# A decoder step on one core: the projection's three groups run as one loop, an exponential is put ahead of weight loads, and a cache copy's 16 runs lie far apart

## The chip, the core and the metric

The kernel runs on one NeuronCore of a Trainium2 chip. TensorE (PE) multiplies into PSUM, VectorE (DVE) and ScalarE (ACT) work elementwise, GpSimd (POOL) copies and broadcasts. SyncE (SP), ACT and POOL issue DMAs, and all of them run on the core's 16 DMA engines. The engines run apart and meet at semaphores. The metric is the device time of one execution in microseconds (us); before the change the median of three runs is 1215.42 us (1214.69 to 1216.04).

## The reference, cut to what matters

One inference step of a two-layer decoder trunk over 256 prompt tokens and 8 sample tokens, width 1024, all in float32:

```
layer 0: u = rms_norm(h)
         z = u @ w_qkv            # 1024 -> 3 groups x (q, k, v) x 16 heads x 64
         q, k = rms_norm per head # v is left as it is
         prompt: banded dilated attention per group, merged over groups
         sample: per group, the new q against 128 cached keys (every 1st, 4th, 16th row
                 of a cache of 128, 512, 2048 rows) and its own k; softmax; times v
         h += merged @ w_o
         new caches = the old caches moved on by one row, the new k and v as last row
layer 1: h += pooling mixer(rms_norm(h))
each layer: route every token to 2 of 16 experts; h += sum of gate * expert(rms_norm(h))
```

The three sample caches are outputs too: 8 samples x (128, 512, 2048) rows x 2 x 1024 floats, each row but the last taken from the input cache one row further on. That is about 176 MB read and written by DMA, with no arithmetic in it.

## The kernel before, in words

**Stages.** In order of time: the norm of the input; the projection; the attention of the 8 samples; the attention of the prompt, one head after another; the product with `w_o`; router and experts of layer 0; the pooling mixer; router and experts of layer 1; the outputs. Each engine has its own program, written out by hand; Python loops are unrolled, `Fori` is a loop on the engine.

**Projection** (PE L1061, ACT L625, DVE L781, POOL L460). A group g has 24 tiles of 128 columns: 8 of q (n = 0 to 7), 8 of k, 8 of v. For a tile PE runs 8 matmuls over the width (L1074); for q and k ACT squares (L629), PE sums the squares per head (L1083), ACT takes the root (L635), DVE the reciprocal and the product (L791, L792); v tiles are only copied (L796). Three tiles behind, PE transposes the result (L1092, L1093) and ACT stores it (L647 to L651); POOL keeps q and k for the prompt's attention (L480). PE, ACT and DVE each run `Fori` over the groups, and a group's body ends when its own last tile is through: PE waits until ACT has stored tile 23 (L1094), DVE until PE has turned it (L805). The next group's tile 0 starts after that. The weights come in chunks of four tiles through three ring slots: SP loads chunk c when PE is done with chunk c - 3 (L372).

**Scores of the samples.** Beside tiles n = 14 to 21, DVE multiplies sample b = n - 14's cached keys with its query, spread over the partitions by POOL, and sums per head (L797 to L804). POOL loads sample b + 4's keys and spreads query b + 2 once sample b is scored (L491 to L496). After the last group, PE adds up the scores (L1103 to L1105) and DVE finds their maximum (L822 to L824).

**Softmax of the samples.** ACT loads the new v rows (L657) and the router's weights (L659, L660: four DMAs whose runs are 4 or 16 floats), and then takes the exponential (L662). DVE divides (L826 to L829), PE turns the result (L1109, L1110), DVE masks it (L832 to L835). PE then adds the new rows' part (`p_newT`, L1114) and the cached values' part in two halves of three loads each (L1123). SP issues half 1's loads into the slots of half 0 as PE frees them (L384).

**Cache copies.** 168 DMAs from the input caches to the output caches: 1, 4 or 16 pieces for each sample. A piece is `[16, y]`: 16 runs of y elements, one for each DMA engine: 65,024, 65,408 or 65,504 bytes by cache. SP puts them between its loads, and a table of counts says how many after which load: L268, here in the order of use:

```
5 and 7 after the first chunks, 3 after each chunk, 2 after each of two value loads of half 0 ("last_chunks"),
2 after half 0, 3, then 1 or 2 per head, 3, 4, 14 before the router, 1 or 2 per expert pair of layer 0,
28 in the pooling stage, 2 per pair of layer 1, the rest (9) after the last expert load
```

SP's queue keeps this order, so a load stands behind the copies issued before it. SP ends when the outputs and all copies have landed (L451, L452).

**Experts** (L1252). Eight pairs of experts per layer; a pair needs six loads of 2 MB (gate, up, down for two experts) in six slots, and a slot's next load is issued when PE has used the old one (L426 to L430).

Of the kernel before, what the change touches and what calls it, by code (L numbers as in the profile page):

```python
# [5 lines left out]
ALU = mybir.AluOpType  # L6
# [4 lines left out]
ds = bass.ds  # L11

P = 128
# [30 lines left out]
def build(nc, x_prompt, x_sample, cache_w128, cache_w512, cache_w2048, state_pool, w_qkv, q_norm,  # L44
# [40 lines left out]
    with ExitStack() as ctx:  # L85
# [251 lines left out]
        def _(sp):  # L337
# [118 lines left out]
        def _(pool):  # L456
# [3 lines left out]
            for g in range(G):  # L460
# [3 lines left out]
                def spread_q(b):  # L464
                    at = 32 * (b // 3 + 1)

                    if b % 2 == 0 and b <= 2:
                        pool.wait_ge(zn_kept, g * NQK + (NQK - 2 + b))
# [7 lines left out]
                for n in range(NQK):  # L476
                    pool.wait_ge(zn_ready, g * NZ + n + 1)
                    if n == KT + 6:
                        pool.wait_ge(q_spread, g * NS + 2)
# [7 lines left out]
                    if n == KT + 5:  # L487
# [20 lines left out]
                pool.wait_ge(rows_sent, g * 16 + 16)  # L508
# [88 lines left out]
        def _(ac):  # L597
# [27 lines left out]
            with ac.Fori(0, G) as g:  # L625
                for s in range(NZ + 4):
                    if s < NQK:
                        ac.wait_ge(z_ready, g * NZ + (s + 1))
                        nc.scalar.activation(zsq[:, s % 2, :], z_bank[s % 4][:, 0:T], ACT.Square).then_inc(zsq_ready, 1)  # L629
                    if 1 <= s <= NQK:  # L630
                        n = s - 1
                        ac.wait_ge(zsum_ready, g * NQK + (n + 1))
                        if n >= 2:
                            ac.wait_ge(zn_ready, g * NZ + (n - 1))
                        nc.scalar.activation(zr[:, n % 2, :], bank[2 + n % 2][:, 0:T], ACT.Sqrt, bias=epsc[:, 0:1],  # L635
                                             scale=1.0 / HD).then_inc(zroot_ready, 1)
                    if s >= 4:
                        n = s - 4
                        what, k = n // KT, n % KT
                        at = slice(k * P, (k + 1) * P)  # L640
                        src = bank[4 + n % 2]
                        if n == 0:
                            ac.wait_ge(tokens_sent, g * (16 * SENT_PER_G) + 16)
                        ac.wait_ge(z_turned, g * NZ + (n + 1))
                        if what == 1:
                            for b in range(2):
                                nc.scalar.activation(k_tok[b][:, at], src[:, b * P:(b + 1) * P], ACT.Copy)  # L647
                        if what == 2:
                            nc.scalar.activation(v_tok[:, :, ds(g, 1), at].rearrange("p b a c -> p (b a) c"),
                                                 src[:, 0:2 * P].rearrange("p (b c) -> p b c", b=2), ACT.Copy)  # L650
                        nc.scalar.activation(qkv_s[0:NS, what, at], src[0:NS, 2 * P:3 * P], ACT.Copy).then_inc(z_stored, 1)  # L651


# [98 lines left out]
        def _(dve):  # L752
# [28 lines left out]
            with dve.Fori(0, G) as g:  # L781
                chain.enter(g, NQK + 1 + NS)
                chain(vec.tensor_copy(gains[:], vecs[:, ds(g * 2 + QK_G, 2)]))
                for n in range(NZ):
                    if n >= 4:
                        dve.wait_ge(z_turned, g * NZ + (n - 3))
                        if n - 4 < NQK:
                            dve.wait_ge(zn_kept, g * NQK + (n - 3))
                    if n < NQK:
                        dve.wait_ge(zroot_ready, g * NQK + (n + 1))  # L790
                        chain(vec.reciprocal(zri[:, n % 2, :], zr[:, n % 2, :]))  # L791
                        vec.scalar_tensor_tensor(out=zn[:, n % 4, :], in0=z_bank[n % 4][:, 0:T], scalar=gains[:, n // KT:n // KT + 1],  # L792
                                                 in1=zri[:, n % 2, :], op0=ALU.mult, op1=ALU.mult).then_inc(zn_ready, 1)
                    else:
                        dve.wait_ge(z_ready, g * NZ + (n + 1))
                        vec.tensor_copy(zn[:, n % 4, :], z_bank[n % 4][:, 0:T]).then_inc(zn_ready, 1)  # L796
                    b = n - (NZ - 2 - NS)  # L797
                    if 0 <= b < NS:
# [612 lines left out]
```

## Time and profile before

| | |
|---|---|
| median of 3 runs | 1215.42 us |
| the profiled execution | 1215.45 us, of it 1213.7 us from the first to the last instruction |
| PE busy | 1090.1 us (90% of the span) |
| DVE, POOL, ACT busy | 434.7, 243.1, 217.1 us |
| DMA | 462.51 MB, mean 381 GB/s |
| the chain that ended last | PE 49%, DMA 14%, DVE 5% |
| 168 copies, issue to landing | medians of 18.4 to 22.1 us by cache |

"Busy" of PE is modelled: its matmuls overlap, and a PE that waits within a stage still shows up as idle only in the rows of that stage. The share of the DMA engines counts the time of their packets, so it may pass 1.00, and a packet that is slowed by others counts for longer. So for DMA the bytes per second of a stretch are read beside its share. Times of rows are us from the start of the span.

### The profile page before, as it was taken

To read this page: it belongs to the slowest core of one execution; us is meant where nothing else is said; L and a number is where in the kernel's file an instruction comes from. 1 tells how busy PE (TensorE), PEld (TensorE's weight loads), DVE (VectorE), ACT (ScalarE), POOL (GpSimd) and SP (SyncE) were. 2 spreads that over 40 slices of the span, in tenths; PEclk is the share of its full clock that TensorE was granted. 3 is DMA by queue.
4 is the path that set the end of the run, shared out by engine and by line. 5 is a ranking of instruction groups with operands and counts; after the bars stand their busy time and mean duration, and the time that the engine had idled before them with its cause. 6 is when DMAs were issued, how large, how long until landed. Compare 5 with 4: busy or idle time off the path is not lost.

```text
span 1213.7 us, 14577 instructions
## 1 busy us (share of the span) xinstructions
PE 1090.1 (90%) x4927; PEld 657.5 (54%) x4927; DVE 434.7 (36%) x843; ACT 217.1 (18%) x532; POOL 243.1 (20%) x504
## 2 busy tenths in 40 slices
PE   7998799999945899997999999998569799999995
PEld 4787588888831588763434444444433344443443
DVE  3455455835840367323112212113851122211212
ACT  2221122222200234212011111112111111111110
POOL 1014202421420122003122222220213221112220
PEclk9999899999976699996999999999678999999998
DMA  9999997999895999999999999999999999999998
GB/s 366 349 382 377 406 364 274 389 372 400 303 370 181 391 344 353 371 355 346 373 430 429 439 416 430 429 438 418 377 331 327 434 424 427 431 429 434 429 432 277
DMA packets 61888, 462.51 MB, mean 381 GB/s; under 512 B 11196, under 2 KB 19148, under 8 KB 46836
## 3 DMA queue, kind: packets, MB, share of 16 engines
q1 hardware_dynamic: 49136, 440.29, 92.4%
q0 software_dynamic: 5424, 18.75, 4.2%
q10 hardware_dynamic: 7284, 2.87, 1.0%
q8 instruction: 30, 0.49, 0.2%
q14 instruction: 14, 0.11, 0.0%
HBM read 454.99 MB, written 183.21 MB: 526 GB/s over the span
## 4 chain that ended last, share of the span: by engine, by line
PE 49%; DMA 14%; DVE 5%; issue 2%; ACTq 1%; ACT 1%; SPq 0%; DVEq 0%; POOLq 0%
PE bank L1262 22%; DMA ring_lo<-in_w_up_dram 12%; PE bank L1232 7%; PE bank L1286 3%; PE bank L1185 2%; DMA ring_lo<-in_cache_kv_w_dram 2%; PE bank L1144 1%; PE bank L1164 1%; PE bank L1241 1%; PE bank L1152 1%; PE bank L1141 1%; PE bank L1248 1%; PE bank L296 1%; PE bank L1192 1%; PE bank L1123 1%
## 5 line engine op out<-in xcount | busy, mean ns | idle before, releaser
L1262 PE MATMUL bank<-ring_lo,scratch 128*64 128x512 f32 x1024 | 340.6, 599 | 11.2 <-DMA ring_lo<-in_w_up_dram 9.3
L1074 PE MATMUL bank<-uT,ring_lo 128*128 128x264 f32 x1152 | 273.7, 392 | 3.2 <-ACT scratch L651 2.7
L1074 PEld LDWEIGHTS bank<-uT,ring_lo 128*128 128x128 f32 x1152 | 218.0, 194 | 43.9 <-issue 4.6
L1262 PE MATMUL bank<-region_a,scratch 128*64 128x512 f32 x512 | 227.8, 598 | 0.0
L1262 PEld LDWEIGHTS bank<-ring_lo,scratch 128*64 128x64 f32 x1024 | 107.0, 138 | 149.7 <-issue 149.3
L791 DVE RECIPROCAL scratch<-scratch 128x264 f32<-128x264 f32 x48 | 86.5, 1802 | 106.0 <-ACT scratch L635 106.0
L1232 PE MATMUL bank<-scratch 128*128 128x512 f32 (+1 forms) x216 | 119.0, 679 | 3.1 <-DVE scratch L947 3.1
L1262 PEld LDWEIGHTS bank<-region_a,scratch 128*64 128x64 f32 x512 | 67.8, 137 | 65.9 <-issue 64.0
L972 DVE TENSOR_TENSOR scratch<-bank,scratch 128x512 f32<-128x512 f32 x16 | 11.1, 692 | 246.8 <-PE bank L1262 246.8
L979 DVE TENSOR_TENSOR hT<-bank,hT 128x264 f32<-128x264 f32 x128 | 55.4, 432 | 120.0 <-PE bank L1286 118.6
L542 POOL TENSOR_TENSOR small<-epsc 128x1 f32<-128x1 f32 x71 | 13.8, 194 | 374.2 <-PE bank L1248 358.8
L1232 PEld LDWEIGHTS bank<-scratch 128*128 128x128 f32 (+1 forms) x216 | 37.7, 201 | 81.1 <-issue 79.5
L480 POOL COPY region_a<-scratch 128x264 f32<-128x264 f32 x48 | 24.6, 512 | 192.1 <-DVE scratch L792 191.8
L1286 PE MATMUL bank<-scratch 128*128 128x264 f32 x256 | 61.2, 392 | 0.0
L556 POOL TENSOR_SCALAR scratch<-slot_no,scratch 128x64 f32<-128x64 f32 (+1 forms) x108 | 60.5, 579 | 0.8 <-issue 0.3
L1286 PEld LDWEIGHTS bank<-scratch 128*128 128x128 f32 x256 | 47.3, 190 | 20.3 <-issue 13.0
L726 ACT ACTIVATE scratch<-bank 128x512 f32<-128x512 f32 x18 | 10.8, 597 | 242.8 <-PE bank L1232 242.8
L629 ACT ACTIVATE scratch<-bank 128x264 f32<-128x264 f32 x48 | 18.7, 391 | 158.5 <-PE bank L1074 145.8
L802 DVE TENSOR_TENSOR ring_lo<-ring_lo,scratch 128x1024 f32<-128x1024 f32 x24 | 40.9, 1706 | 14.9 <-POOL scratch L472 7.9
L562 POOL TENSOR_SCALAR scratch<-slot_no,scratch 128x64 f32<-128x64 f32 (+1 forms) x108 | 44.8, 430 | 0.0
L472 POOL PARTITION_BROADCAST scratch<-scratch x24 | 33.0, 1373 | 37.6 <-DVE scratch L803 23.7
L740 ACT ACTIVATE scratch<-bank 128x512 f32<-128x512 f32 x32 | 19.1, 597 | 93.3 <-PE bank L1262 93.3
(226 smaller groups left out, 1116.7 us busy)
## 6 DMA issues: line engine op xcount, KB each, us to landing
out_dram<-in_cache_kv_w_dram SPq DMA_DIRECT2D x128, 1023.5 KB, 22.1
ring_lo<-in_w_up_dram SPq DMA_DIRECT2D x32, 2048.0 KB, 22.4
ring_lo<-in_w_qkv_dram SPq DMA_DIRECT2D x18, 2048.0 KB, 17.1
ring_lo<-in_w_gate_dram SPq DMA_DIRECT2D x16, 2048.0 KB, 14.7
region_a<-in_w_down_dram SPq DMA_DIRECT2D x16, 2048.0 KB, 15.2
region_a<-in_w_gate_dram SPq DMA_DIRECT2D x16, 2048.0 KB, 19.9
ring_lo<-in_w_down_dram SPq DMA_DIRECT2D x16, 2048.0 KB, 19.4
out_dram<-in_cache_kv_w_dram SPq DMA_DIRECT2D x32, 1022.0 KB, 18.4
```

The costliest lines, as they stand in the source:

```text
L472: nc.gpsimd.partition_broadcast(q_rep[b % 2][:, :], q_row[at:at + 1, b % 3, :], channels=P).then_inc(q_spread, 1)
L480: nc.gpsimd.tensor_copy(qk[:, g, n // KT, n % KT, :], zn[:, n % 4, :]).then_inc(zn_kept, 1)
L556: last = nc.gpsimd.tensor_scalar(pick_gate[0:n, b, e * CAP:(e + 1) * CAP], slot_no[0:n, :], pair_at[0:n, 0, b, e:e + 1], pair_at[0:n, 1, b ...
L562: last = nc.gpsimd.tensor_scalar(pick[0:n, b, e * CAP:(e + 1) * CAP], slot_no[0:n, :], pair_at[0:n, 0, b, e:e + 1], None, ALU.is_equal)
L791: chain(vec.reciprocal(zri[:, n % 2, :], zr[:, n % 2, :]))
L802: chain(vec.tensor_tensor(k_tile, k_tile, q_rep[b % 2][:, :], ALU.mult))
L979: vec.tensor_tensor(hT[:, m, :], spread_bank[m % 4][:, 0:T], hT[:, m, :], ALU.add).then_inc(spread_added, 1)
L1074: last = mm(z_bank[s % 4][:, 0:T], w[:, k, at:at + P], uT[:, k, :], start=(k == 0), stop=(k == KT - 1))
L1185: last = mm(bank[m % 2][:, 0:T], w[:, f % 4, m * P:(m + 1) * P], oT[:, f, :], start=(f == 0), stop=(f == KT - 1))
L1232: last = mm(bank[a][:, :], made[0:sizes[b], b, :], u_tok[0:sizes[b], b, a * 512:(a + 1) * 512], start=(b == 0), stop=(b == 2))
L1262: last = mm(out[rows, :], lhs[:, k, rows], weights[e][w][:, k, columns], start=(k == 0), stop=(k == k_tiles - 1))
L1286: mm(spread_bank[m % 4][:, 0:T], y_pair[:, m * P:(m + 1) * P], place, start=True, stop=True).then_inc(spread, 1)
```

## The change

The projection's `Fori` loops become one unrolled loop over 72 tiles on PE, ACT and DVE. Tile i's buffers are chosen by i, so that tile 0 of the next group follows tile 23, and the transposes, roots and stores of a group's last tiles come after the first matmuls of the next. The waits at a group's end go; ACT waits for the transfers that read its token buffers only where it writes them again. The scores of sample b move from tile n = 14 + b to n = 16 + b, and POOL spreads the queries one tile later.

ACT takes the samples' exponential ahead of the loads of the new v rows and the router's weights. PE adds the new rows' part between the two halves, as eight matmuls of 32 columns in place of two of 128. POOL no longer waits for its own store of v before it stores the new cache row.

"last_chunks" goes from 2 to 3, so two more copies are issued at the end of the projection, and 7 in place of 9 are left for the end. A copy piece is cut differently: for the cache of 2048 rows, its 16 runs began 65,504 bytes apart, and now begin 16 x 65,504 = 1,048,064 bytes apart; for 512 rows 65,408 and now 261,632; for 128 rows there is one piece per sample and nothing changes. The bytes of a piece and its 16 runs stay as long as they were.

```diff
-        COPIES = {"first_chunks": 7, "chunk": (3, 3, 3), "last_chunks": 2, "sample_half": (2, 0), "head": (1, 2), "heads_end": 3,
+        COPIES = {"first_chunks": 7, "chunk": (3, 3, 3), "last_chunks": 3, "sample_half": (2, 0), "head": (1, 2), "heads_end": 3,
...
-                moved.append([v[0].rearrange("b l w h e -> b (l w h e)")[:, at:at + m].rearrange("b (n x y) -> b n x y", n=n, x=16)
+                moved.append([v[0].rearrange("b l w h e -> b (l w h e)")[:, at:at + m].rearrange("b (x n y) -> b n x y", n=n, x=16)
...
-                pool.wait_ge(rows_sent, g * 16 + 16)
...
-            with ac.Fori(0, G) as g:
-                for s in range(NZ + 4):
+            for i in range(TILES + 4):
...
+                    if n % NZ == KT:
+                        ac.wait_ge(tokens_sent, g * (16 * SENT_PER_G) + 16)
...
+            ac.wait_ge(s_rows_ready, 1)
+            nc.scalar.activation(s_rows[:, :, :], s_rows[:, :, :], ACT.Exp, bias=small[:, 36:37],
+                                 accum_out=small[:, 37:38]).then_inc(s_exp_ready, 1)
             ac.wait_ge(rows_sent, 16 * G)
...
-            ac.wait_ge(s_rows_ready, 1)
-            nc.scalar.activation(s_rows[:, :, :], s_rows[:, :, :], ACT.Exp, bias=small[:, 36:37],
-                                 accum_out=small[:, 37:38]).then_inc(s_exp_ready, 1)
...
-                    b = n - (NZ - 2 - NS)
-                    if 0 <= b < NS:
+                b = n - (NZ - NS)
+                if b >= 0:
...
-                dve.wait_ge(z_turned, g * NZ + NZ)
-                dve.wait_ge(zn_kept, g * NQK + NQK)
...
-            with pe.Fori(0, G) as g:
-                for s in range(NZ + 3):
+            for i in range(TILES + 3):
...
-                pe.wait_ge(z_stored, g * NZ + NZ)
...
-            pe.wait_ge(v_new_landed, 16)
-            for a in range(2):
-                mm(bank[3 + a][:, :], p_newT[0:G * NS, :], v_new[0:G * NS, a * 512:(a + 1) * 512], start=True, stop=False)
...
+                if half == 0:
+                    pe.wait_ge(v_new_landed, 16)
+                    for a in range(2):
+                        for b4 in range(HALF):
+                            rows = slice(b4 * 2 * H, (b4 + 1) * 2 * H)
+                            mm(bank[3 + a][rows, :], p_newT[0:G * NS, rows], v_new[0:G * NS, a * 512:(a + 1) * 512], start=False, stop=False)
```

PE at the end of a group, before: the last tile's matmuls (L1074), the transposes of the tiles still under way (L1092, L1093), and the branch back that waits for ACT's last store.

```order
L1074 MATMUL bank7<-uT,ring_lo 128x264 [waits zn_ready]
L1074 MATMUL bank7<-uT,ring_lo 128x264 x7
L1086 REGISTER_ALU
L1092 MATMUL bank4<-ident,scratch 128x128 [waits z_stored,zn_ready]
...
L1092 MATMUL bank5<-ident,scratch 128x128 [waits z_stored,zn_ready]
L1092 MATMUL bank5<-ident,scratch 128x128
L1093 MATMUL bank5<-ident,scratch 8x128
L1061 REGISTER_ALU [waits z_stored]
L1061 COMPARE_AND_BRANCH
```

The same place now (the matmuls are L1082, the transposes L1100 and L1101, the sum of squares L1091):

```order
L1082 MATMUL bank7<-uT,ring_lo 128x264 [waits zn_ready]
L1082 MATMUL bank7<-uT,ring_lo 128x264 x7
L1100 MATMUL bank4<-ident,scratch 128x128 [waits z_stored,zn_ready]
L1100 MATMUL bank4<-ident,scratch 128x128
L1101 MATMUL bank4<-ident,scratch 8x128
L1082 MATMUL bank0<-uT,ring_lo 128x264 [waits zn_ready,ring_full0]
L1082 MATMUL bank0<-uT,ring_lo 128x264 x7
L1100 MATMUL bank5<-ident,scratch 128x128 [waits z_stored,zn_ready]
L1100 MATMUL bank5<-ident,scratch 128x128
L1101 MATMUL bank5<-ident,scratch 8x128
```

Tile 0 of the next group (bank0) now stands between the transposes of the last tiles, and no branch or wait for the last store stands ahead of it.

ACT after the projection, before: the load of the new v rows (L657), four loads of router weights, then the table load and the exponential of the samples' scores (L662).

```order
L657 DMA scratch<-v_of_samples 24x1024 [waits z_turned,zn_kept,rows_sent]
L659 DMA wr<-in_router_group_w_dram 128x8x4
L660 DMA wr<-in_router_expert_w_dram 128x8x16
L659 DMA wr<-in_router_group_w_dram 128x8x4
L660 DMA wr<-in_router_expert_w_dram 128x8x16
L662 ACT_TABLE_LOAD
L662 ACTIVATE rstd,small<-rstd,small 128x387 [waits s_rows_ready]
```

And now:

```order
L664 ACT_TABLE_LOAD
L664 ACTIVATE rstd,small<-rstd,small 128x387 [waits s_rows_ready]
L669 DMA scratch<-v_of_samples 24x1024 [waits z_turned,zn_kept,rows_sent]
L671 DMA wr<-in_router_group_w_dram 128x8x4
L672 DMA wr<-in_router_expert_w_dram 128x8x16
L671 DMA wr<-in_router_group_w_dram 128x8x4
L672 DMA wr<-in_router_expert_w_dram 128x8x16
```

The table load and the exponential have moved past five DMAs; the table load itself waits for nothing.

PE in the samples' attention, before: the turned probabilities (L1109, L1110), the new rows' part (L1114), and the first matmuls of half 0 (L1123).

```order
L1109 MATMUL bank1<-ident,rstd 128x128 x2
L1110 MATMUL bank2<-ident,ring_lo 24x128
L1114 MATMUL bank3<-scratch,ring_lo 128x512 [waits v_new_landed,p_keys_ready]
L1114 MATMUL bank4<-scratch,ring_lo 128x512
L1123 MATMUL bank3<-ring_lo 32x512 [waits ring_full0]
```

And now, up to the first load of half 1 (L1128 is L1123 of before, L1136 the new rows' part):

```order
L1118 MATMUL bank2<-ident,ring_lo 24x128
L1128 MATMUL bank3<-ring_lo 32x512 [waits ring_full0,p_keys_ready]
...
L1128 MATMUL bank4<-ring_lo 32x512 x4
L1136 MATMUL bank3<-scratch,ring_lo 32x512 [waits v_new_landed]
L1136 MATMUL bank3<-scratch,ring_lo 32x512 x3
L1136 MATMUL bank4<-scratch,ring_lo 32x512 x4
L1128 MATMUL bank3<-ring_lo 32x512 [waits ring_full0]
```

The new rows' part has moved behind all of half 0, and with it the wait for the new v rows.

## Rows read from the trace of the kernel before

**Rows 1.** The page: busy tenths of PE and DMA, and GB/s, in 40 slices.

```profile
PE   7998799999945899997999999998569799999995
...
DMA  9999997999895999999999999999999999999998
GB/s 366 349 382 377 406 364 274 389 372 400 303 370 181 391 344 353 371 355 346 373 430 429 439 416 430 429 438 418 377 331 327 434 424 427 431 429 434 429 432 277
```

**Rows 2.** Five stretches: length, busy of PE, PEld, DVE, ACT, POOL; PE clock, DMA share, GB/s.

```profile
150.00:240.00 90.00, 90.00 (x429) 75.88 (x428) 61.33 (x55) 20.83 (x71) 22.50 (x31) 1.00 0.92 349
325.00:404.00 79.00, 47.32 (x232) 26.90 (x230) 24.91 (x39) 6.03 (x19) 12.24 (x18) 0.73 0.82 295
425.00:500.00 75.00, 73.38 (x530) 62.66 (x529) 49.37 (x171) 32.35 (x93) 15.79 (x22) 0.99 1.01 342
860.00:920.00 60.00, 40.77 (x139) 23.35 (x141) 31.47 (x106) 11.00 (x22) 10.53 (x28) 0.72 1.00 335
965.00:1171.00 206.00, 201.60 (x852) 86.41 (x852) 37.36 (x72) 27.51 (x42) 41.89 (x108) 0.99 1.01 429
```

**Rows 3.** PE's order of time in the projection: start, length, line; idle before, its releaser.

```profile
92.99 3.73 PE L1074 MATMUL bank<-uT,ring_lo 128*128 128x264 f32 x16
...
97.32 3.73 PE L1074 MATMUL bank<-uT,ring_lo 128*128 128x264 f32 x16
...
101.21 3.73 PE L1074 MATMUL bank<-uT,ring_lo 128*128 128x264 f32 x16
...
109.62 4.81 PE L1074 MATMUL bank<-uT,ring_lo 128*128 128x264 f32 x16
...
114.60 3.73 PE L1074 MATMUL bank<-uT,ring_lo 128*128 128x264 f32 x16
...
122.38 3.73 PE L1074 MATMUL bank<-uT,ring_lo 128*128 128x264 f32 x16
...
127.19 3.73 PE L1074 MATMUL bank<-uT,ring_lo 128*128 128x264 f32 x16
...
139.92 10.33 PE L1074 MATMUL bank<-uT,ring_lo 128*128 128x264 f32 x32 [1.35 <-ACT scratch L651]
...
150.54 3.72 PE L1074 MATMUL bank<-uT,ring_lo 128*128 128x264 f32 x16
...
236.82 3.73 PE L1074 MATMUL bank<-uT,ring_lo 128*128 128x264 f32 x16
...
251.59 3.72 PE L1074 MATMUL bank<-uT,ring_lo 128*128 128x264 f32 x16
```

**Rows 4.** DVE's order of time: the first score of group 0.

```profile
103.06 2.20 DVE L802 TENSOR_TENSOR ring_lo<-ring_lo,scratch 128x1024 f32<-128x1024 f32 x1 [7.35 <-POOL scratch L472]
```

**Rows 5.** DVE's order of time: either side of the samples' exponential.

```profile
354.93 0.15 DVE L824 TENSOR_SCALAR small<-small 128x1 f32<-128x1 f32 x1
369.04 0.16 DVE L826 RECIPROCAL small<-small 128x1 f32<-128x1 f32 x1 [13.95 <-ACT rstd L662]
```

**Rows 6.** ACT's order of time there (ACTq: its queue issues a DMA).

```profile
354.14 9.30 ACTq L659 DMA_DIRECT2D wr<-in_router_group_w_dram  x1
...
367.00 1.28 ACT L662 ACT_TABLE_LOAD   x1 [20.83 <-issue]
```

**Rows 7.** PE's order of time in the samples' attention.

```profile
372.26 3.77 PE L1114 MATMUL bank<-scratch,ring_lo 24*128 24x512 f32 x4 [0.90 <-DVE ring_lo L835]
375.96 8.06 PE L1123 MATMUL bank<-ring_lo 128*32 128x512 f32 x48
...
392.42 3.23 PE L1123 MATMUL bank<-ring_lo 128*32 128x512 f32 x16 [2.38 <-DMA ring_lo<-in_cache_kv_w_dram]
397.54 1.92 PE L1123 MATMUL bank<-ring_lo 128*32 128x512 f32 x16 [1.88 <-DMA ring_lo<-in_cache_kv_w_dram]
```

**Rows 8.** Waits of the whole run: us in total, times, longest.

```profile
PE bank L1262 <- DMA ring_lo<-in_w_up_dram: 9.3, 5, 5.1
```

**Rows 9.** Waits of SP's queue, in the same form.

```profile
SPq L452 <- DMA out_dram<-in_cache_kv_w_dram: 7.7, 1, 7.7
```

More of the change, by code:

```diff
@@ L465, in spread_q @@
                     at = 32 * (b // 3 + 1)
[L467 to L468 removed]
+                    if b in (0, 2):
+                        pool.wait_ge(zn_kept, g * NQK + (NQK if b else NQK - 1))
                     if b >= 1:
@@ L622, in _ @@
             ac.wait_ge(bias_stored, 16)
-            with ac.Fori(0, G) as g:
-                for s in range(NZ + 4):
[L627 to L651, printed above, removed]
@@ new lines, in _ @@
+            for i in range(TILES + 4):
+                if i < TILES and i % NZ < NQK:
+                    ac.wait_ge(z_ready, i + 1)
+                    nc.scalar.activation(zsq[:, i % 2, :], z_bank[i % 4][:, 0:T], ACT.Square).then_inc(zsq_ready, 1)
+                if 1 <= i <= TILES and (i - 1) % NZ < NQK:
+                    q = qk_count(i - 1)
+                    ac.wait_ge(zsum_ready, q + 1)
+                    if q >= 2:
+                        ac.wait_ge(zn_ready, tiles_until(q - 1))
+                    nc.scalar.activation(zr[:, q % 2, :], bank[2 + q % 2][:, 0:T], ACT.Sqrt, bias=epsc[:, 0:1],
+                                         scale=1.0 / HD).then_inc(zroot_ready, 1)
+                if i >= 4:
+                    n = i - 4
+                    g, what, k = n // NZ, n % NZ // KT, n % KT
+                    at = slice(k * P, (k + 1) * P)
+                    src = bank[4 + n % 2]
+                    if n % NZ == 0 and g:
+                        ac.wait_ge(q_rows_landed, g * 48)
+                    if n % NZ == KT:
+                        ac.wait_ge(tokens_sent, g * (16 * SENT_PER_G) + 16)
+                        if g:
+                            ac.wait_ge(rows_sent, g * 16)
+                    ac.wait_ge(z_turned, n + 1)
+                    if what == 1:
+                        for b in range(2):
+                            nc.scalar.activation(k_tok[b][:, at], src[:, b * P:(b + 1) * P], ACT.Copy)
+                    if what == 2:
+                        nc.scalar.activation(v_tok[:, :, g, at], src[:, 0:2 * P].rearrange("p (b c) -> p b c", b=2), ACT.Copy)
+                    nc.scalar.activation(qkv_s[0:NS, what, at], src[0:NS, 2 * P:3 * P], ACT.Copy).then_inc(z_stored, 1)
@@ new lines, in _ @@
+            for i in range(TILES + 3):
+                if i < TILES:
+                    g, s = divmod(i, NZ)
+                    c = s // TPC
+                    if s % TPC == 0:
+                        pe.wait_ge(ring_full[c % 3], g * 32 + 16 * (c // 3 + 1))
+                    if i >= 4:
+                        pe.wait_ge(zn_ready, i - 3)
+                    w = slot(c % 3).rearrange("p (k n) -> p k n", k=KT)
+                    at = s % TPC * P
+                    for k in range(KT):
+                        if i == 0:
+                            pe.wait_ge(u_ready, k + 1)
+                        last = mm(z_bank[i % 4][:, 0:T], w[:, k, at:at + P], uT[:, k, :], start=(k == 0), stop=(k == KT - 1))
+                    last.then_inc(z_ready, 1)
+                if i == 2:
+                    pe.wait_ge(bias_copied, 1)
+                if 1 <= i <= TILES and (i - 1) % NZ < NQK:
+                    q = qk_count(i - 1)
+                    pe.wait_ge(zsq_ready, q + 1)
+                    if q >= 2:
+                        pe.wait_ge(zroot_ready, q - 1)
+                    mm(bank[2 + q % 2][:, 0:T], blockones[:], zsq[:, q % 2, :], start=True, stop=True).then_inc(zsum_ready, 1)
+                if i >= 3:
+                    n = i - 3
+                    pe.wait_ge(zn_ready, n + 1)
+                    if n >= 2:
+                        pe.wait_ge(z_stored, n - 1)
+                    dst = bank[4 + n % 2]
+                    if n % NZ >= KT:
+                        for b in range(2):
+                            nc.tensor.transpose(dst[:, b * P:(b + 1) * P], zn[:, n % 4, b * P:(b + 1) * P], ident[:])
+                    nc.tensor.transpose(dst[0:NS, 2 * P:3 * P], zn[:, n % 4, SEQ:T], ident[:]).then_inc(z_turned, 1)
@@ L1123, in _ @@
                             last = mm(bank[3 + a][rows, :], p_masked[:, half, g, rows], slot(g)[:, at:at + 512],
-                                      start=False, stop=(half == 1 and g == G - 1))
+                                      start=(half == 0 and g == 0), stop=(half == 1 and g == G - 1))
                     last.then_inc(pv_s_ready, 1)
+                if half == 0:
[4 more added lines that the diff above has]
+                            mm(bank[3 + a][rows, :], p_newT[0:G * NS, rows], v_new[0:G * NS, a * 512:(a + 1) * 512], start=False, stop=False)
             pe.wait_ge(o_own_ready, 1)
```

89 lines of the change are left out of this document (33 added, 56 removed).

## The prediction

> **What bounds the kernel now.** I read the page's 40 slices first, then the stretches, then the order of time at each place that the change touches, then the waits. PE is busy in nearly every slice, and so is DMA: its digit is 9 almost throughout, while its rate goes from 181 to 439 GB/s [rows 1]. So a stretch is judged by its rate, and by who waits in it. In the projection's middle PE is busy for all 90.00 us and DMA has room: share 0.92, 349 GB/s [rows 2]. In the samples' attention neither is full: PE 47.32 of 79 us at a mean clock of 0.73, DMA 0.82 and 295 GB/s [rows 2]; this is a chain of waits. In the prompt's attention DMA is full at 342 GB/s with PE at 73.38 of 75 us. In the pooling stage, where SP has issued 28 copies in a row, DMA is full at 335 GB/s. In layer 1 it is full at 429 GB/s with one copy among each few expert loads, and PE is busy for 201.60 of 206 us [rows 2]. PE's waits for expert loads come to 9.3 us in the whole run, in five waits [rows 8]: PE sets the pace there, with DMA right behind it. Two questions follow: how much earlier the front part ends, and whether the copies keep their rate.
>
> **Projection without drains.** What is lost is read from the distances between the starts of tiles. A tile with a sum of squares and v transposes takes 97.32 - 92.99 = 4.33 us, a v tile 101.21 - 97.32 = 3.89 [rows 3]. In group 0 the v tile at 101.21 is followed only at 109.62 (4.52 too late), the next at 114.60 (1.09), and the one at 122.38 at 127.19 (0.92). The first is a score's doing: DVE stood 7.35 us for POOL's spread query [rows 4], and tiles queue behind it. With the scores two tiles later, 2 x 4.33 = 8.66 us, that wait is covered; DVE's work of a score also leaves the k tiles, where the reciprocal stands beside it. The first group's end: from 127.19 (tile 23) to 150.54 (tile 2 of the next) are 23.35 us, where unbroken tiles take 3.89 + 3.89 + 4.33 = 12.11; 11.24 go, a part of it the 10.33 us that the first two tiles after the stop take where two unbroken ones take 3.89 + 3.89 [rows 3]. The second end: 251.59 - 236.82 = 14.77, less 12.11 is 2.66. Sum 4.52 + 1.09 + 0.92 + 11.24 + 2.66 = 20.4; I take 20, since v transposes done in the drain now stand beside q tiles. The last group ends as before: its last score is later by two tiles, but now is all that DVE has left to do. POOL reaches the next group's tile 0 only after it has sent the last group's tokens, some tiles late; DVE needs it from tile 4 on. If that fails, a part of the 11.24 comes back.
>
> **The exponential.** DVE hands over the scores at 354.93 + 0.15 = 355.08 and goes on at 369.04, 13.96 us later [rows 5]. ACT was issuing the router's loads: one of them holds its queue for 9.30 us, and its table load starts at 367.00 [rows 6]. Now the table load waits for nothing and lies in ACT's idle time; what stays is 369.04 - 367.00 - 1.28 = 0.76, with the hand-over about 1. Gain 13.0 (11.7 if the table load comes after the wait). Moved along are five DMAs on ACT's queue: the new v rows, wanted only after half 0, and the router's weights, wanted only after the whole attention of the prompt. No ACT work waits behind them before the prompt's attention.
>
> **The new rows' part behind half 0.** Half 0 now starts 375.96 - 372.26 = 3.70 us earlier after the turned probabilities [rows 7]. Its eight small matmuls come where PE waits for half 1's loads anyway (it waits 2.38 and 1.88 us for the second and third of them [rows 7]), so I cost them at nothing; without that cover they cost the same 3.70.
>
> **What the DMAs take back.** Front gain so far 20 + 13.0 + 3.7 = 36.7. The same bytes and two more copies must then pass in that much less time. Half 1's third load lands 397.54 - 392.42 = 5.12 us after its second, 2.097 MB at 410 GB/s [rows 7]: these loads run at full rate, and PE waits for them. Low bound of the loss: if the stretches 150 to 240 and 325 to 404 could run at the 429 GB/s of layer 1, their 90 x 349 + 79 x 295 = 54.7 MB would take 128 of their 169 us, which leaves 41 us of room for 36.7 and two copies of 2.4 (1.048 MB at 429): nothing is lost. High bound: their rates stay, and only idle DMA time is room, 0.08 x 90 + 0.18 x 79 = 21.4 us: 36.7 + 4.9 - 21.4 = 20 are lost. I take 6, near the low end, because every earlier load of the projection is issued eight tiles ahead of its use and can slip; half 1's cannot, and stands behind two copies (4.9) and, for about 1 us, among the router's short runs.
>
> **The end.** SP waits 7.7 us for the last copies after the outputs [rows 9]. Two of the nine copies left for the end move forward. At the 335 GB/s of an unbroken row of copies one takes 1.048 / 0.335 = 3.13 us, so 6.3 of the 7.7 go.
>
> **The runs far apart.** No row of before shows a copy in this layout. Bytes, runs per engine and run length stay. Bounds: every row of copies at 429 GB/s, where single copies run, or down to 181 GB/s, the slowest slice [rows 1]. I take no change, 335, by the nearest row, the copies themselves. What the ends are worth is worked out below.
>
> **Sum.** 36.7 - 6 + 6.3 = 37.0. The profiled execution took 1215.45 us, 0.03 over the median of three, so the forecast is 1215.45 - 37.0 = 1178.4 us. From the samples' attention on, each copy and load is issued when PE or DVE is at a certain place, so these stages move forward as a whole. What comes last next is PE's last pair and the outputs.
>
> **Rival 1: the DMAs are full.** The 20 us of the high bound are lost: 36.7 - 20 + 6.3 = 23, time 1192. For it: shares of 0.92 and more in the projection. Against it: its rates of 349 and 295 GB/s lie far under 429.
>
> **Rival 2: far apart is faster.** If rows of copies ran at 429, the 28 of the pooling stage would save 28 x (3.13 - 2.44) = 19 us of DMA, but only waits can go: PE's 9.3 [rows 8] and the remaining 7.7 - 6.3 = 1.4 of the end. Time 1168. For it: 335 is well under the 429 that the same engines reach. Against: nothing shows that the layout is why; an unbroken row of copies also reads and writes DRAM at once.
>
> **Rival 3, the other side: far apart is slower.** Sixteen engines then work at addresses 1 MiB less 512 bytes apart, for reads and writes. Copies that run in rows are exposed, since loads that PE waits for queue behind them: 28 in the prompt's attention (3 + 18 + 3 + 4), 14 before the router, 28 in pooling, 7 at the end: 77 x 3.13 = 241 us. Slower by a part f, this adds 241 x f. The gain of 37.0 is used up at f = 0.154, that is below 335 / 1.154 = 290 GB/s. At f = 0.25 (268 GB/s) the time is 1178.4 + 60.3 = 1239; at the far bound of 181 GB/s, f = 0.85, it would be 1383. For it: DMA is full in those stretches, so nothing hides it. Against: the third load of half 1 takes its rows 16 cache rows of 8 KB apart, 128 KiB, and keeps 410 GB/s [rows 7]; but it only reads, and at an eighth of the distance.
>
> The Trainium skill, "DMA: Bandwidth & Descriptors", section "Latency and other measured facts", speaks for this rival: DMA copies whose rows lie large powers of two apart lose rate, 207 GB/s at 512 KiB and 164 at 2 MiB against a full 214, and a small padding of 192 bytes did not help. An estimate from that page, halfway between the two at 1 MiB, is f = 0.15, and the sum by it would be 1178.4 + 37 = 1215, no change at all. No run here shows that distance.
>
> **How the numbers follow.** Forecast 0.45, with a range of its own of 1171 to 1187 (the loss 0 to 14). Rival 1 0.15. Rival 2 0.13. Copies slower but over 290 GB/s, times from 1187 to 1213, 0.10. Rival 3 0.17. The range is 1165 to 1213: it leaves out most of rival 3 and a little under rival 2. A measurement of this kernel can tell about 0.2%, 2.4 us, from no change. Faster by more: 0.45 + 0.15 + 0.13 and 0.08 of the 0.10 are 0.81. Within: 0.02 + 0.02 = 0.04. Slower: 0.15.
>
> **What would show it.** Projection: starts of tiles 3.9 to 4.3 us apart across both group ends, no low clock there, tile 2 of the second group near 133 instead of 150.54, that of the third near 231 instead of 251.59. If tiles 4 to 8 of a group start late with DVE waiting for POOL, the drain has only moved. Exponential: DVE's wait for ACT near 1 us instead of 13.95. Half 0 some 37 us earlier, and PE's waits for half 1 longer than 2.38 and 1.88 by the 6 I take; if by 20, rival 1. The end: SP's last wait for copies under 2 us. The layout: the pooling stage's rate at 335 GB/s; at 400 or more rival 2; under 290 rival 3, with PE's waits for expert loads well over 9.3 us. My forecast is wrong above all if that one number moves.

## The result and the profile after

The changed kernel takes 1227.19 us (median of nine runs, 1221.54 to 1238.31) against 1216.04 for the kernel before beside it. The ratio is 1.0095, 95% interval 1.0061 to 1.013: slower by 11 us (7 to 16 by the interval), where 37 us less were forecast. The profiled execution took 1222.90 us, its span 1221.1.

The page of the changed kernel, in the form of [rows 1]:

```profile
PE   6999999999747998969799999997579399999997
...
DMA  9999999999999999999999999999999999999997
GB/s 364 353 382 377 397 420 374 384 406 368 363 366 392 311 308 324 334 351 254 411 430 428 430 429 430 428 435 407 278 280 278 413 430 426 429 430 429 426 441 243
```

Its five stretches, in the form of [rows 2]:

```profile
150.00:240.00 90.00, 90.00 (x433) 75.97 (x432) 58.22 (x53) 20.13 (x73) 18.37 (x27) 1.00 1.01 389
325.00:404.00 79.00, 50.90 (x233) 27.87 (x234) 20.47 (x64) 8.69 (x21) 9.57 (x16) 0.59 1.02 360
425.00:500.00 75.00, 69.68 (x454) 59.62 (x453) 35.84 (x124) 24.17 (x72) 9.74 (x14) 0.95 0.98 335
860.00:920.00 60.00, 45.88 (x169) 24.66 (x171) 25.91 (x91) 12.14 (x23) 14.94 (x41) 0.75 0.99 278
965.00:1171.00 206.00, 198.73 (x832) 83.24 (x829) 33.92 (x64) 25.93 (x40) 35.41 (x92) 0.98 1.01 429
```

The projection's rate rose from 349 to 389 GB/s. The pooling stage's fell from 335 to 278 with the DMA engines as busy as before. The slices of the prompt's attention (311, 308, 324) and the one in which the 14 copies issued ahead of the router pass (254) are low too. Where single copies stand among expert loads, 429 GB/s stayed.

The projection did what the prediction said. PE's starts at tiles 25 and 26, and 49 and 50 (the group ends of [rows 3]; tiles are counted from 0):

```profile
128.54 3.73 PE L1082 MATMUL bank<-uT,ring_lo 128*128 128x264 f32 x16
132.87 3.73 PE L1082 MATMUL bank<-uT,ring_lo 128*128 128x264 f32 x16
...
227.27 3.73 PE L1082 MATMUL bank<-uT,ring_lo 128*128 128x264 f32 x16
231.61 3.73 PE L1082 MATMUL bank<-uT,ring_lo 128*128 128x264 f32 x16
```

Tile 26 starts at 132.87 (150.54 before; "near 133" was foretold) and tile 50 at 231.61 (251.59; "near 231"): 19.98 us gained for the 20 taken. The exponential's wait on DVE (L832 and L834 were L824 and L826 of [rows 5]) is now 0.78 us in place of 13.95:

```profile
337.41 0.15 DVE L832 TENSOR_SCALAR small<-small 128x1 f32<-128x1 f32 x1
338.34 0.16 DVE L834 RECIPROCAL small<-small 128x1 f32<-128x1 f32 x1 [0.78 <-ACT rstd L664]
```

Where the gain went is read from five places in PE's order of time: half 0's start, half 1's third load, the product with `w_o`, the pooling mixer's norm behind layer 0's last pair, and the last transposes. The changed kernel:

```profile
341.56 8.07 PE L1128 MATMUL bank<-ring_lo 128*32 128x512 f32 x48 [0.90 <-DVE ring_lo L843]
...
363.05 3.64 PE L1128 MATMUL bank<-ring_lo 128*32 128x512 f32 x16 [11.56 <-DMA ring_lo<-in_cache_kv_w_dram]
...
373.82 3.64 PE L1128 MATMUL bank<-ring_lo 128*32 128x512 f32 x16 [1.74 <-DMA ring_lo<-in_cache_kv_w_dram]
...
486.90 28.75 PE L1196 MATMUL bank<-uT,ring_lo 128*128 128x264 f32 x128 [0.54 <-ACT uT L687]
...
835.83 3.80 PE L305 MATMUL bank<-scratch,ones 128*128 128x264 f32 x16 [0.89 <-ACT scratch L311]
...
1209.87 2.81 PE L1352 MATMUL bank<-ident,hT 128*128 128x128 f32 x24 [0.53 <-ACT scratch L740]
```

The kernel before at the last three of them (the first two stand in [rows 7], 375.96 and 397.54):

```profile
503.72 28.75 PE L1185 MATMUL bank<-uT,ring_lo 128*128 128x264 f32 x128 [0.54 <-ACT uT L679]
...
841.70 3.80 PE L296 MATMUL bank<-scratch,ones 128*128 128x264 f32 x16 [0.90 <-ACT scratch L302]
...
1198.42 2.81 PE L1341 MATMUL bank<-ident,hT 128*128 128x128 f32 x24 [0.53 <-ACT scratch L732]
```

So the changed kernel is ahead by 34.4 us at half 0, 23.7 at half 1's third load, 16.8 at `w_o` and 5.9 at the pooling norm, and at the end it is 11.45 behind. It loses where copies follow each other and in the first expert pairs behind them, and holds its place, to some 3 us, among the other pairs. Part of the losses is named among its waits (us in total, times, longest), in the form of [rows 8]:

```profile
PE bank L1273 <- DMA region_a<-in_w_gate_dram: 25.9, 2, 19.9
...
PE bank L1128 <- DMA ring_lo<-in_cache_kv_w_dram: 15.1, 3, 11.6
...
PE bank L1273 <- DMA ring_lo<-in_w_up_dram: 11.1, 7, 3.2
DVE small L862 <- DMA ring_lo<-bias_by_distance: 6.5, 3, 3.4
```

The kernel before waited for a gate load once:

```profile
PE bank L1262 <- DMA region_a<-in_w_gate_dram: 1.9, 1, 1.9
```

PE's waits for `w_up` hardly grew (9.3 before), those for half 1's loads from 7.5 to 15.1. The waits for gate loads went from 1.9 to 25.9 us; 19.92 of it, at 964.44, is for a load that SP issues behind the 28 pooling copies. DVE's waits for bias loads, which stand between the copies of the heads, are new. SP's wait for the last copies went to 3.4 us from 7.7 [rows 9], not to the 1.4 foretold:

```profile
SPq L461 <- DMA out_dram<-in_cache_kv_w_dram: 3.4, 1, 3.4
```

### The profile page after: what moved, and what is told of

Read it like the earlier page. It is cut to its first block, busy times and chain, and to the rows that moved or that the text cites. A ratio compares the mean times of both kernels' runs of the same rounds, so it can differ in the third digit from the quotient of the medians.

```text
span 1221.1 us, 14097 instructions
## 1 busy us (share of the span) xinstructions
PE 1088.0 (89%) x4939; PEld 655.2 (54%) x4939; DVE 432.3 (35%) x843; ACT 216.2 (18%) x532; POOL 239.8 (20%) x504
## 4 chain that ended last, share of the span: by engine, by line
PE 40%; DMA 24%; DVE 6%; issue 2%; SPq 1%; ACT 1%; another core or an unknown queue 0%; ACTq 0%; DVEq 0%
PE bank L1273 20%; DMA ring_lo<-in_w_up_dram 14%; PE bank L1243 6%; DMA region_a<-in_w_gate_dram 4%; DMA ring_lo<-bias_by_distance 4%; DMA ring_lo<-in_cache_kv_w_dram 3%; PE bank L1297 3%; PE bank L1196 2%; PE bank L1128 1%; PE bank L1252 1%; PE bank L305 1%; PE bank L1259 1%; PE bank L1155 1%; PE bank L1203 1%; SPq L363 1%
## 5 line engine op out<-in xcount | busy, mean ns | idle before, releaser
L1273 PE MATMUL bank<-ring_lo,scratch 128*64 128x512 f32 x1024 | 348.7, 607 | 37.1 <-DMA region_a<-in_w_gate_dram 25.9
L1082 PE MATMUL bank<-uT,ring_lo 128*128 128x264 f32 x1152 | 269.9, 388 | 0.5 <-DVE uT L319 0.5
L1082 PEld LDWEIGHTS bank<-uT,ring_lo 128*128 128x128 f32 x1152 | 214.6, 191 | 38.9 <-issue 1.2
L1273 PE MATMUL bank<-region_a,scratch 128*64 128x512 f32 x512 | 235.4, 614 | 0.0
L1273 PEld LDWEIGHTS bank<-ring_lo,scratch 128*64 128x64 f32 x1024 | 109.8, 140 | 181.0 <-issue 180.7
L489 POOL COPY region_a<-scratch 128x264 f32<-128x264 f32 x48 | 19.2, 409 | 165.8 <-DVE scratch L801 165.6
## 6 DMA issues: line engine op xcount, KB each, us to landing
region_a<-in_w_down_dram SPq DMA_DIRECT2D x16, 2048.0 KB, 16.8
```

The lines of the kernel that those rows point to most:

```text
L489: nc.gpsimd.tensor_copy(qk[:, g, n // KT, n % KT, :], zn[:, n % 4, :]).then_inc(zn_kept, 1)
L1082: last = mm(z_bank[i % 4][:, 0:T], w[:, k, at:at + P], uT[:, k, :], start=(k == 0), stop=(k == KT - 1))
L1273: last = mm(out[rows, :], lhs[:, k, rows], weights[e][w][:, k, columns], start=(k == 0), stop=(k == k_tiles - 1))
```

## The experiments

Theory: a row of copies moves at 278 in place of 335 GB/s because the 16 runs of a copy lie 1 MiB less 512 bytes apart; by the prediction's 241 us of exposed copies, 335/278 - 1 = 0.205 of it is 49 us. Rivals: the unrolled front part pushes the DMA work together; the front's other steps gained less than was taken. Every kernel is the changed one with one more edit, unless the text says otherwise. All times are medians beside runs of the kernel before (1215.25 to 1220.62 us by series), so ratios compare best. "Pooling" is the rate from 870 to 910 us, in the middle of the 28 copies (925 to 965 in `s2_before_far`).

| kernel | runs of the large cache lie apart | us | ratio to before, 95% | pooling, GB/s |
|---|---|---|---|---|
| before | 65,504 B | 1217.57 | 1 | 332 |
| changed | 1,048,064 B | 1227.19 | 1.0095 [1.0061, 1.013] | 278 |
| s1_side | 65,504 B | 1180.79 | 0.9706 [0.9682, 0.9729] | 328 |
| s2_before_far (before, new cut alone) | 1,048,064 B | 1266.55 | 1.0394 [1.0331, 1.0457] | 269 |
| s3_pitch512 | 524,032 B | 1192.11 | 0.9783 [0.976, 0.9805] | 312 |
| s4_pitch256 | 262,016 B | 1181.86 | 0.9705 [0.9686, 0.9723] | 330 |
| t1_near | 16,376 B | 1184.33 | 0.9734 [0.9705, 0.9763] | 327 |
| r1_read_far | read 1,048,064, written 65,504 | 1196.96 | 0.9854 [0.9803, 0.9904] | 305 |
| r2_write_far | read 65,504, written 1,048,064 | 1202.62 | 0.9892 [0.9849, 0.9936] | 304 |
| r3_pitch15 | 982,560 B (15 copies of 16) | 1187.27 | 0.9719 [0.9697, 0.9741] | 323 |
| r4_pitch12 | 786,048 B (12 copies of 16) | 1187.32 | 0.9723 [0.9703, 0.9743] | 325 |
| r5_less4k | 1,044,480 B | 1237.23 | 1.0161 [1.0132, 1.0189] | 256 |
| r6_less16k | 1,032,192 B | 1213.93 | 0.9979 [0.9961, 0.9998] | 294 |
| b1_exp_back | 65,504 B | 1190.60 | 0.9782 [0.9747, 0.9816] | 338 |
| t2_router_early | 65,504 B | 1183.89 | 0.9705 [0.9688, 0.9722] | 324 |
| t3_copies_later | 65,504 B | 1186.03 | 0.972 [0.9704, 0.9737] | 331 |

**The cut alone, taken out and put in.** `s1_side`:

```diff
-... .rearrange("b (x n y) -> b n x y", n=n, x=16)
+... .rearrange("b (n x y) -> b n x y", n=n, x=16)
```

> The changed kernel with the 16 runs of a piece side by side again. Theory (the distance of 1,048,064 bytes slows copies that run in rows): the pooling stage goes back from 278 to about 335 GB/s, the waits for the bias loads and PE's wait of 25.9 us for the gate load behind the pooling copies go, and the time is 1227 less about 45, some 1182 us (1175 to 1192). Rival (the unrolled front part only pushes the DMA work together, and the rate fell because more wants to pass at once): the pooling stage, which has the same 28 copies in a row in either case, stays near 278, and the time stays within 10 us of 1227.

`s2_before_far` makes the opposite edit in the kernel before.

> The kernel before with the new cut of the copies alone. Theory: pooling at 278 instead of 335 GB/s; at a loss of a fifth on the copies in rows (77 and 2 more at the end, 3.13 us each) about 1216 + 50 = 1266 us if all of it is exposed, and no less than 1245. Rival (the layout costs little, the earlier front collides): 1216 to 1225 us, pooling at 335.

Both came as the theory had them: 46 us less without the cut, 49 us more with it alone. The rival, that the earlier front part pushes the DMA work together, falls: the rate falls with the cut in either front part. The pooling stage of `s1_side`, then of `s2_before_far`:

```profile
870.00:910.00 40.00, 37.53 (x116) 14.19 (x118) 7.62 (x27) 4.34 (x7) 14.86 (x41) 0.79 0.98 328
```

```profile
925.00:965.00 40.00, 32.55 (x114) 13.82 (x114) 9.44 (x46) 4.79 (x8) 14.84 (x41) 0.79 0.99 269
```

DMA's share is the same in both; the bytes per second are not. `s1_side` keeps its lead to the end (the five places again, and the only wait for a gate load, 1.76 us in place of the 19.92):

```profile
340.69 7.09 PE L1128 MATMUL bank<-ring_lo 128*32 128x512 f32 x48 [0.90 <-DVE ring_lo L843]
...
366.83 1.92 PE L1128 MATMUL bank<-ring_lo 128*32 128x512 f32 x16 [1.88 <-DMA ring_lo<-in_cache_kv_w_dram]
...
471.36 28.75 PE L1196 MATMUL bank<-uT,ring_lo 128*128 128x264 f32 x128 [0.54 <-ACT uT L687]
...
810.36 3.80 PE L305 MATMUL bank<-scratch,ones 128*128 128x264 f32 x16 [0.89 <-ACT scratch L311]
...
922.97 0.61 PE L1273 MATMUL bank<-ring_lo,scratch 128*64 128x512 f32 x1 [1.76 <-DMA region_a<-in_w_gate_dram]
...
1168.39 2.81 PE L1352 MATMUL bank<-ident,hT 128*128 128x128 f32 x24 [0.53 <-ACT scratch L740]
```

Ahead by 35.3, 30.7, 32.4, 31.3 and 30.0 us. SP's wait at the end:

```profile
SPq L461 <- DMA out_dram<-in_cache_kv_w_dram: 0.9, 1, 0.9
```

**How far apart.** `s3_pitch512`, and `s4_pitch256` with 4 in place of 8 (pieces are then indexed by both k and n):

```diff
-... .rearrange("b (x n y) -> b n x y", n=n, x=16)
+... .rearrange("b (k x n y) -> b k n x y", k=n // apart, n=apart, x=16)   # apart = n if n < 16 else 8
```

> The changed kernel with the runs of the large cache 524,032 bytes apart (half the distance). Theory, if the loss grows with the distance: the pooling stage between 278 and 335, about 305 GB/s, and about 1205 us. Rival (any distance but side by side is as bad): 278 GB/s and 1227 us. Rival (1 MiB alone is bad): 335 GB/s and 1182 us.

> The same at 262,016 bytes. Theory: near 325 to 335 GB/s in the pooling stage and 1180 to 1190 us, since the copies of the middle cache, whose runs are 261,632 bytes apart, kept the mean time of their packets. Rival (any distance is as bad): 278 GB/s and 1227 us.

Half the distance costs 11 us (1192.11 - 1180.79) over `s1_side`, a quarter nothing to be told apart. `s4_pitch256` leaves the middle cache's runs 261,632 bytes apart, so the whole loss is the large cache's.

```profile
870.00:910.00 40.00, 32.00 (x116) 13.43 (x114) 10.55 (x52) 6.07 (x10) 14.84 (x41) 0.83 1.01 312
```

That is `s3_pitch512`, between the two levels; `s4_pitch256` is at the upper one:

```profile
870.00:910.00 40.00, 37.27 (x130) 14.92 (x132) 7.70 (x28) 4.66 (x7) 14.90 (x41) 0.86 1.00 330
```

`t1_near` goes the other way:

```diff
-... .rearrange("b (x n y) -> b n x y", n=n, x=16)
+... .rearrange("b (n z x y) -> b n x z y", n=n, x=16, z=4)
```

> The changed kernel with the runs nearer still: each engine copies four runs of 16,376 bytes that lie 262,016 bytes apart, and the 16 engines start 16,376 bytes apart (the middle cache: 16,352). If nearness goes on paying, rows of copies run faster than 333 GB/s: at 380 GB/s the 77 copies in rows give back 77 x 0.37 = 28 us of DMA, of which PE's waits for loads and the front part's waits can return some 10, so 1171 us. If the gain ends at 262,016 bytes, as the equal times at 65,504 and 262,016 bytes say, or if shorter runs cost, it is 1181 us or more.

No gain: 327 GB/s. About 330 is what a row of copies reaches from 16 KB to a quarter of a MiB.

**Reading or writing.** In `r1_read_far` only the source is cut far apart, in `r2_write_far` only the destination:

```diff
-... .rearrange("b (x n y) -> b n x y", n=n, x=16) for v, at in ((out, 0), (src, 2 * D))
+... .rearrange(cut, n=n, x=16) for v, at, cut in ((out, 0, "b (n x y) -> b n x y"), (src, 2 * D, "b (x n y) -> b n x y"))
```

> The changed kernel; copies read runs far apart and write them side by side (rows of a cache then land in other places than the reference's; the bytes, the runs and their length are the same). Theory a (the distance hurts reading): as the changed kernel, 1227 us and 278 GB/s in the pooling stage. Theory b (it hurts writing): as with all side by side, 1181 us and 333 GB/s. Theory c (both alike): between, about 1204 us and 305 GB/s.

> The other half: copies read side by side and write far apart (rows land in other places). Theory a (reading): 1181 us and 333 GB/s in the pooling stage. Theory b (writing): 1227 us and 278 GB/s. Theory c (both alike): about 1204 us and 305 GB/s. If each half costs nothing, the distance must be on both sides at once.

Both sides lose alike, theory c, with times somewhat under its 1204. The stretches of `r1_read_far` and `r2_write_far`:

```profile
870.00:910.00 40.00, 31.99 (x119) 14.92 (x119) 11.79 (x62) 8.27 (x14) 14.92 (x41) 0.74 0.98 305
```

```profile
870.00:910.00 40.00, 31.99 (x134) 14.69 (x132) 11.64 (x62) 8.27 (x14) 14.90 (x41) 0.83 1.02 304
```

A copy of 1.048 MB costs 3.20 us at 328, 3.44 and 3.45 at 305 and 304, and 3.77 at 278: the two losses of 0.24 and 0.25 make up most of the 0.57. The times say the same: over `s1_side`, by the ratios, 18 and 23 us for one side each and 47 for both.

**Distance or power of two.** `r3_pitch15` and `r4_pitch12` (12 in place of 15) cut a sample's 256 runs in blocks:

```diff
+far = v[b, 0:16 * 15 * y].rearrange("(x n y) -> n x y", n=15, x=16)
+side = v[b, 16 * 15 * y:m].rearrange("(n x y) -> n x y", x=16, y=y)
```

> The changed kernel; of the large cache's 256 runs per sample, 240 go in 15 copies with their 16 runs 15 x 65,504 = 982,560 bytes apart, the last 16 in one copy side by side. If the distance as such slows a row of copies (half a MiB cost 11 us, a MiB 46), 0.94 MiB costs about 40: 1220 us and 285 GB/s in the pooling stage. If it is the power of two (16 runs that all start at nearly the same place within a MiB), this distance is as good as side by side: 1181 us and 333 GB/s.

> The same with 12 copies of runs 12 x 65,504 = 786,048 bytes apart, and four side by side. Distance as such: between half a MiB and a MiB, of three copies in four, about 1205 us and 300 GB/s in pooling. Power of two: as 262,016 bytes, since multiples of 12/16 MiB come to four places within a MiB, 1182 us and 333 GB/s.

It is not the distance as such. At 0.94 MiB, nearly the same distance, the kernel is within 0.2% of `s1_side`, and 323 GB/s is close to 328:

```profile
870.00:910.00 40.00, 35.91 (x113) 15.15 (x114) 7.38 (x35) 3.67 (x6) 14.91 (x41) 0.70 1.00 323
```

Left open was how near to a MiB is too near. `r5_less4k`, and `r6_less16k` with 16384 in place of 4096:

```diff
-m = (src.shape[2] - 1) * 2 * D
+m = 16 * (2 ** 18 - 4096 // 4) if n == 16 else (src.shape[2] - 1) * 2 * D   # the rest of a sample: one small copy at the end
```

> The changed kernel; the large cache's runs are 65,280 bytes long and 1 MiB less 4,096 bytes apart; the 57,344 bytes left of each sample go in one more small copy each at the end (8 in all). If it is enough that the 16 starts differ by 4 KiB steps: 333 GB/s in the pooling stage, and 1181 us and up to 6 more for the small copies. If the starts must be spread over the whole MiB: 278 GB/s and about 1227 us. The Trainium skill (DMA: Bandwidth & Descriptors, Latency and other measured facts) has a pitch of 4 MiB restored to full rate by 4 KiB more, and not by 192 bytes; by that, the first.

> The same with 64,512 bytes and 1 MiB less 16,384. If the loss falls off step by step with the offset: between r5 and 333 GB/s. If 4 KiB are enough already: as r5, 1181 to 1187 us. If even this is too near: 278 GB/s, 1227 us.

4 KiB do not help, against the expectation's first case; the rate is even lower, for which no run shows a reason, and 16 KiB give back a part (the times hold the eight small copies too: SP's last wait for copies is 7.4 and 10.3 us here, 3.4 in the changed kernel):

```profile
870.00:910.00 40.00, 25.59 (x104) 17.14 (x105) 25.76 (x92) 8.67 (x18) 0.00 (x0) 0.76 1.01 256
```

```profile
870.00:910.00 40.00, 32.33 (x124) 15.51 (x123) 11.85 (x62) 8.27 (x14) 14.94 (x41) 0.74 1.00 294
```

So with runs of 64 KB the rate is lowest where the 16 starts, counted within a MiB, differ by 512 or 4,096 bytes from one to the next; with 16,384 it is higher, and with 66,016 (`r3_pitch15`) close to side by side. Two places within a MiB (`s3_pitch512`) cost 5% of the rate, four (`s4_pitch256`, `r4_pitch12`) nothing to be told apart. That only the place within a MiB counts is a reading that fits these distances; no distance over a MiB was tried. The Trainium skill, "DMA: Bandwidth & Descriptors", section "Latency and other measured facts", has full rate back at 4 KiB of padding, for tiles of 16 KiB rows at a pitch of 4 MiB; here, at 1 MiB and with runs of 64 KB, 4 KiB gave 256 GB/s, and the measurement decides for this case. It calls lock-stepped streams on the same HBM channels an inference. These runs fit that, and don't prove it: no row shows a channel.

**The front part's own steps.** `b1_exp_back` is `s1_side` with the exponential (L663 to L665) behind the router weights' loads:

> The changed kernel with the runs side by side and the exponential put back behind the router weights' loads. The exponential's step was priced at 13.0 us. If it is worth that in the chain, 1181 + 13 = 1194 us, with half 0 about 13 us later; since the loads for half 1 then have more time, up to 5 us of it may be hidden: 1189 to 1194. If the front part is bound by the DMAs alone, 1181 to 1184.

Half 1's third load starts at 379.62 us in place of 366.83, so the step is worth 12.8 there (13.0 taken):

```profile
379.62 3.35 PE L1128 MATMUL bank<-ring_lo 128*32 128x512 f32 x16 [1.48 <-DMA ring_lo<-in_cache_kv_w_dram]
```

At the end some 9 are left (0.9782 - 0.9706 = 0.0076 of 1217; the two intervals allow some 5 us either way). That the later start gives transfers time which the earlier one lacks would explain it; this was not shown by itself.

In `s1_side` half 1's loads land 15.2 us after their issue, in the kernel before 10.0 (the median of three is the last number; `s1_side` first):

```profile
ring_lo<-in_cache_kv_w_dram SPq DMA_DIRECT2D x3, 2048.0 KB, 15.2
```

```profile
ring_lo<-in_cache_kv_w_dram SPq DMA_DIRECT2D x3, 2048.0 KB, 10.0
```

Two reasons for it were tried, `t2_router_early` (the loads of L671 and L672 issued at `i in (28, 52)` of ACT's projection loop) and `t3_copies_later`:

```diff
-"sample_half": (2, 0)
+"sample_half": (0, 2)
```

> The changed kernel with its runs side by side, and the router weights' four loads issued within the projection (tiles 28 and 52) in place of after the exponential. Theory (half 1's loads now land 15.2 us after their issue against 10.0 before, because the router weights' short runs pass at that time): they land in about 10 us, half 1 ends 4 to 5 us earlier, time about 1176 us. Rival (half 1 stands behind two copies): no change, 1181. If the short runs disturb the projection's chunk loads, 1183 or more.

> The changed kernel with its runs side by side, and the two copies that stand ahead of half 1's loads put behind them. Theory (the router weights' short runs delay half 1): within 2 us of 1181. Rival, as the prediction had it (two copies of 2.4 us stand ahead): half 1 ends up to 4.9 us earlier, 1176 us.

Neither gains in time. Half 0 and half 1's third load start here in `t2_router_early` (first) and `t3_copies_later` (second):

```profile
345.63 7.03 PE L1129 MATMUL bank<-ring_lo 128*32 128x512 f32 x48 [0.90 <-DVE ring_lo L844]
...
370.41 1.92 PE L1129 MATMUL bank<-ring_lo 128*32 128x512 f32 x16 [1.48 <-DMA ring_lo<-in_cache_kv_w_dram]
```

```profile
343.15 7.76 PE L1128 MATMUL bank<-ring_lo 128*32 128x512 f32 x48 [0.90 <-DVE ring_lo L843]
...
366.02 3.64 PE L1128 MATMUL bank<-ring_lo 128*32 128x512 f32 x16 [2.10 <-DMA ring_lo<-in_cache_kv_w_dram]
```

These can't be set against `s1_side`'s 340.69 and 366.83 as they stand, since the executions differ by up to 4 us at tile 3 of the projection already, ahead of either edit. Tile 3 in `s1_side`, `t2_router_early` and `t3_copies_later`:

```profile
36.61 3.72 PE L1082 MATMUL bank<-uT,ring_lo 128*128 128x264 f32 x16
```

```profile
40.65 3.72 PE L1083 MATMUL bank<-uT,ring_lo 128*128 128x264 f32 x16
```

```profile
36.75 3.72 PE L1082 MATMUL bank<-uT,ring_lo 128*128 128x264 f32 x16
```

Counted from there, half 1's third load starts after 330.2, 329.8 and 329.3 us, so neither edit moves it by as much as 1 us, and the expectation of 4 to 5 us by a single culprit fell both times. That the sum of the bytes sets the place, whichever transfer stands last, would fit; it was not shown by itself. Half 0's start says nothing of either edit: counted from tile 3 it lies at 304.1, 305.0 and 306.4 us in these three, and at 301.6 in `r3_pitch15`, which changes nothing there but the copies' cut.

The fastest version is `s1_side`: the change without its new cut, 3.8% under the changed kernel (0.9706 / 1.0095) and 2.9% under the kernel before.

## Why the prediction was wrong

**The step that failed: the runs far apart.** The prediction said "I take no change, 335, by the nearest row, the copies themselves". That row is of copies with runs side by side, and the layout was the very thing that changed; the runs showed 278. The miss follows from it: 241 us of exposed copies by 0.205 is 49 us, and 46 (`s1_side`) and 49 (`s2_before_far`) were measured. Rival 3 had the mechanism, the total and the break-even right (under 290 GB/s the gain is gone; `r6_less16k` at 294 came out at 0.998 of the kernel before, with its small copies) and was given 0.17; the prediction itself names the pooling rate as the number on which the forecast hangs. That the total fits so well is in part luck. From `s1_side` to the changed kernel, by the five places, the prompt's attention lost 8.5 us where 28 copies by the same price are 18; up to half 1's third load 7.0 were lost, where the price had nothing (1.9 of them lie ahead of the projection's tile 3, which starts at 36.61 in the one execution and 38.48 in the other); router and layer 0 lost 9.9 for 9, pooling and layer 1 16.0 for 18, the last copies 2.5 for 4.5. The rival's two arguments were weighed wrongly. That DMA is full in those stretches, for it, held. Half 1's third load, against it, reads at an eighth of the distance, and `s4_pitch256` shows that even a quarter says nothing of a MiB. The rule of the Trainium skill ("DMA: Bandwidth & Descriptors", "Latency and other measured facts") pointed to f = 0.15 and 1215 us; the runs gave 0.205 and 1227, so it was nearer than the row.

**The sum without that step was right.** `s1_side` is the change as the prediction priced it: 1180.79 us for 1178.4, its own range 1171 to 1187. Single terms fit less closely than the sum:

- Projection without drains: 20 taken, 19.98 measured at tile 50. The foretold danger, that DVE waits for POOL instead, did not come: its first score waits 5.71 us (7.35 in [rows 4]), but no tile behind it is late.

```profile
106.28 1.23 DVE L811 TENSOR_TENSOR ring_lo<-ring_lo,scratch 128x1024 f32<-128x1024 f32 x1 [5.71 <-POOL scratch L481]
```

- The exponential: 13.0 taken, 13.2 of the wait gone in the trace, 12.8 at half 1 and some 9 at the end by `b1_exp_back`.
- What the DMAs take back: 6 taken. In `s1_side` the lead at half 1's third load is 30.7 of the 36.7, so 6.0 at sight; but 1.8 of this lead stand already at tile 3, which starts at 36.61 and in the kernel before at 38.38. Counted from tile 3, 7.8 were taken back: 3.2 before half 0, where DVE's waits for cached keys are 16.5 us in place of 6.9 (that they are the cause is not shown), and the rest at half 1. In the changed kernel, with tile 3 at 38.48, it was 13.0, since copies slowed down there too. The place was half wrong: the two copies ahead of half 1 alone are not the reason (`t3_copies_later`).

```profile
38.38 3.72 PE L1074 MATMUL bank<-uT,ring_lo 128*128 128x264 f32 x16
```

- The new rows' part behind half 0: it lies in PE's wait for half 1, as costed. It was not tried by itself.
- The end: 6.3 taken, 7.7 - 0.9 = 6.8 in `s1_side`; with slow copies only 4.3.

**Of the rivals**, 1 (DMAs full, 1192) and 2 (far apart faster, 1168) did not happen: `s1_side` lies 11 us under the first, and no cut moved a row of copies clearly faster than side by side.

## What to carry to other kernels

When an edit changes where a transfer's parallel runs start, the trace of the old layout has no row for it: don't take the old rate as the nearest row. Look at how many different places within a MiB the starts take (here one place cost 15% of the rate, two 5%, four nothing), and price both rates over all transfers that others wait behind. In a stage where the DMA share is near 1.00, read bytes per second before and after, since the share does not show the loss. Bundled with others, such an edit hides their gain by its price; one run with it taken out tells both.

## What the runs showed that was not expected

- Sixteen runs of 64 KB that start 1 MiB less 512 bytes apart move at 278 GB/s, 1 MiB less 4 KiB at 256, less 16 KiB at 294, less 64.5 KiB at 323, side by side at 324 to 338 by kernel.
- The rate falls only where copies follow each other: among expert loads the stretch from 965 to 1171 us keeps 429 GB/s in the changed kernel, with its copies cut far apart.
- Reading and writing far apart cost alike (305 and 304 GB/s against 328), and the two losses nearly add up (278 for both).
